# Three low-part subtractions of the attention output weights, on GpSimd instead of VectorE

## The reference, cut to what matters

```
q = (h @ w_q + b_q)                      # 16 heads of 64
logits = q k^T / 8 + bias;  masked to a window of 128
m = max(logits.max(-1), sink);  p = exp(logits - m)
probs = p / (p.sum(-1) + exp(sink - m))
o = probs @ v
mix = o @ w_o + b_o                      # w_o: 1024 x 1024
hs = hs + rms_norm(mix, norm_mix_post);  then the ffn with w_gate_up
```

## Time and profile before

| | us |
|---|---|
| median of 3 runs | 987.18 |
| lowest and highest | 986.81, 991.97 |
| the profiled execution | 991.97 |
| its span | 990.2 |
| mean granted clock of PE | 0.987 of full speed |

### The profile page before, as it was taken

One profiled execution on the slowest core, in us unless ns is written; L12 is line 12 of the kernel. 1 busy time (PEld: TensorE's weight loads), 2 busy tenths in 40 slices (PEclk: granted clock), 3 DMA queues, 4 the chain that ended last, 5 costly groups with the idle time before them and its releaser, 6 DMA issues.

```text
span 990.2 us, 16804 instructions
## 1 busy us (share of the span) xinstructions
PE 956.9 (97%) x6905; PEld 799.6 (81%) x6905; DVE 521.1 (53%) x927; ACT 413.3 (42%) x688; POOL 181.9 (18%) x246
## 2 busy tenths in 40 slices
PE   6999999999999999999999999989899999999985
PEld 5899999998978899999998999778754554554465
DVE  3645544436895655555446648774623333323266
ACT  4543333436686633434456456753311111111172
POOL 4033333111002233333120422201200000000013
PEclk8999999999999999999999999999899999999998
DMA  8444453457813344543563431129389999999901
GB/s 312 171 153 183 173 185 117 175 165 221 175 69 126 130 170 173 189 171 125 181 244 150 177 128 48 48 90 390 132 334 415 422 422 420 422 421 422 419 40 43
DMA packets 37213, 211.76 MB, mean 214 GB/s; under 512 B 2576, under 2 KB 16160, under 8 KB 18080
## 3 DMA queue, kind: packets, MB, share of 16 engines
q1 hardware_dynamic: 37152, 210.91, 55.8%
HBM read 209.83 MB, written 1.07 MB: 213 GB/s over the span
## 4 chain that ended last, share of the span: by engine, by line
PE 89%; DVE 4%; ACT 3%; issue 2%; DMA 1%; POOL 1%; SPq 0%; DVEq 0%; POOLq 0%; ACTq 0%
PE ps L1387 50%; PE ps L1861 11%; PE ps L1875 6%; PE ps L1884 3%; PE ps L1379 2%; PE ps L1833 2%; PE ps L1315 2%; PE ps L1834 2%; PE ps L1404 1%; PE ps L1538 1%; PE ps L1604 1%; PE ps L1323 1%; PE ps L1470 1%; DMA ring<-in_w_pool 1%; PE ps L1796 1%
## 5 line engine op out<-in xcount | busy, mean ns | idle before, releaser
L689 DVE TENSOR_TENSOR wl<-ring,wh 128x2048 fp32r<-128x2048 f32 (+3 forms) x103 | 204.6, 1988 | 173.6 <-ACT wh L808 173.5
L808 ACT ACTIVATE wh<-ring 128x2048 fp32r<-128x2048 f32 (+3 forms) x103 | 171.2, 1665 | 249.3 <-PE ps L1387 246.5
L1387 PE MATMUL ps<-xh,wh 128*128 128x256 f32 (+3 forms) x591 | 167.8, 284 | 0.7 <-DVE xl L2471 0.7
L1387 PE MATMUL ps<-xl,wh 128*128 128x256 f32 (+3 forms) x591 | 166.4, 282 | 0.0
L1387 PE MATMUL ps<-xh,wl 128*128 128x256 f32 (+3 forms) x591 | 166.4, 282 | 0.0
L1387 PEld LDWEIGHTS ps<-xh,wh 128*128 128x128 f32 (+3 forms) x591 | 109.3, 185 | 2.2 <-issue 1.3
L1387 PEld LDWEIGHTS ps<-xh,wl 128*128 128x128 f32 (+3 forms) x591 | 109.4, 185 | 0.1
L1387 PEld LDWEIGHTS ps<-xl,wh 128*128 128x128 f32 (+3 forms) x591 | 109.4, 185 | 0.0
L1387 PE MATMUL ps<-acth,wh 128*128 128x272 f32 (+1 forms) x352 | 100.4, 285 | 0.0
L1387 PE MATMUL ps<-acth,wl 128*128 128x272 f32 (+1 forms) x352 | 100.2, 285 | 0.0
L1387 PE MATMUL ps<-actl,wh 128*128 128x272 f32 (+1 forms) x352 | 99.9, 284 | 0.0
(11 more groups left out here) (450 smaller groups left out, 1863.3 us busy)
## 6 DMA issues: line engine op xcount, KB each, us to landing
wring<-in_w_eg SPq DMA_DIRECT2D x32, 2048.0 KB, 14.3
ring<-in_w_gu SPq DMA_DIRECT2D x22, 2048.0 KB, 7.5
wring<-in_w_ed SPq DMA_DIRECT2D x16, 2048.0 KB, 12.6
ring<-in_w_dn SPq DMA_DIRECT2D x16, 1408.0 KB, 5.8
ring<-in_w_z SPq DMA_DIRECT2D x7, 2048.0 KB, 7.6
ring<-in_w_out SPq DMA_DIRECT2D x4, 1152.0 KB, 5.1
ring<-in_w_q SPq DMA_DIRECT2D x8, 512.0 KB, 6.5
ring<-in_w_o SPq DMA_DIRECT2D x8, 512.0 KB, 15.3
```

The lines of the kernel that those rows point to most:

```text
L689: ins = dve.tensor_tensor(to, src, h.bitcast(F32), ALU.subtract)
L808: ins = act.activation(to, src, ACT.Copy)
L1387: ins = mm(o, p, q, start=first and n == 0, stop=last and n == 2)
```

## The change

`split_lo` gets a number of parts; with 8 parts a piece is made by eight subtractions of 256 columns, and the last one counts lo_done. POOL makes the low parts of w_o pieces 0, 1 and 2 in this way, after its sums for ffnpost0; it waits first until all pieces ahead of w_o are made. DVE no longer makes these three. It makes piece 3 as before, in one instruction, and waits first until lo_done has counted pieces 0 to 2.

```diff
-        def split_lo(dve, name, slot, rnd, i, j, size):
+        def split_lo(dve, name, slot, rnd, i, j, size, parts=1):
...
-            for (to, src), (h, _) in zip(parts_of(name, low, w, size), parts_of(name, high, w, size)):
-                ins = dve.tensor_tensor(to, src, h.bitcast(F32), ALU.subtract)
+            if parts > 1:
+                n = size // parts
+                for q in range(parts):
+                    at = slice(q * n, (q + 1) * n)
+                    ins = dve.tensor_tensor(low[:, at], w[:, at], high[:, at].bitcast(F32), ALU.subtract)
+            else:
+                for (to, src), (h, _) in zip(parts_of(name, low, w, size), parts_of(name, high, w, size)):
+                    ins = dve.tensor_tensor(to, src, h.bitcast(F32), ALU.subtract)
             ins.then_inc(sem("lo_done"), 1)
...
             sum_chunks(pool, "ffnpost0", T)
+            pool.wait_ge(sem("lo_done"), NUMBER["w_o", 0])
+            for x in [*halves("w_o", 0, PIECE), halves("w_o", 1, PIECE)[0]]:
+                split_lo(pool, "w_o", *x, parts=8)
             sum_chunks(pool, "mixpost1", SEQ)
...
-                if u == 2:
-                    split_lo(dve, "w_o", *halves("w_o", 0, PIECE)[0])
                 if u + 2 < HEAD_PAIRS:
                     logits(u + 2)
                 if u >= 2:
                     attended_low(u - 2)
-            split_lo(dve, "w_o", *halves("w_o", 0, PIECE)[1])
-            attended_low(HEAD_PAIRS - 2)
-            split_lo(dve, "w_o", *halves("w_o", 1, PIECE)[0])
-            attended_low(HEAD_PAIRS - 1)
+            for u in range(HEAD_PAIRS - 2, HEAD_PAIRS):
+                attended_low(u)
+            dve.wait_ge(sem("lo_done"), NUMBER["w_o", 3])
             split_lo(dve, "w_o", *halves("w_o", 1, PIECE)[1])
```

## The result

The changed kernel is slower: 997.51 us in the median of four runs (996.64 to 1000.77) beside 988.08 us for the kernel before in the same series (986.81 to 991.97). The ratio is 1.0089 with a 95% interval of 1.0065 to 1.0113. A second series, with the changed kernel timed again, gave 1.0088 (1.0064 to 1.0112). The forecast was 990.3 us, with 985.5 to 995.5 as its range. The sign was right; the forecast growth, 3.1 us, is a third of the measured 9.4 us.

A forecast was written before the change was run, and what follows sets the result against it. PE was taken to bound the attention stretch, with DVE's multiplications needed in time. Hits of 1.27 + 1.02 + 1.02 us less 0.23 us gave +3.1 us on the 987.18 us median: 990.3 us, range 985.5 to 995.5 us.

The forecast's parts named there:

- What bounds, and what the relief is worth: Attention of the first block: PE bounds; of 6.85 us taken from DVE, at most 0.23 us is gained, before logits(4).
- POOL's times, the waits and the load: POOL takes 5.9 us a piece, none late; DVE's added wait loses nothing; the earlier w_gu1 tile 1 load is booked zero.
- The hits: DVE's short instructions in pairs 0, 3 and 6 are delayed by POOL's: 1.27 + 1.02 + 1.02 us on the path.
- The price of a hit: Each DVE instruction meeting one of POOL's loses 0.36 us, the mean of two delays in the last stage.
- The upper bound that I had given: A hit on a DVE instruction costs at most 0.42 us; 24 hits on the path would cost 10.1 us.
- The cover: Slack before PE starts second heads: 0.71 us in pair 0, 0.24 us in pair 6, the latter also taken for pair 3.
- For piece 0: POOL's work from 269.9 us hits pair 0: 1.98 us of hits, 0.71 us covered, 1.27 us on the path.
- For piece 1: POOL's work from 282.6 us, four hits before pair 3's heads: 1.26 us, of which 1.02 us on the path.
- For piece 2: POOL's work from 295.9 us, four instructions fall on pair 6: 1.26 us of hits, 0.24 us covered, 1.02 us on the path.
- the granted clock of 1.00: Around the first block's attention the granted clock was read as 1.00, the 2.4 GHz level; no term was booked for it.
- Rival A: POOL holds DVE off for its whole instruction: 0.74 us a hit in pairs 0, 3 and 6, +7.8 us, 995.0 us; chance 0.20.
- Its own sign: Rival A would show as groups of four L2277 multiplications on DVE lasting over 3 us while POOL runs.

The follow-up runs named there:

- e1: The changed kernel, but POOL subtracts only 8 columns of each of the three pieces and the rest is left out; ratio to the kernel before 0.9985.
- e3: As e1 (8 columns of each piece on POOL), but w_o piece 0 whole on POOL in eight subtractions; 989.59 us, run once.
- e4: As e1 (8 columns of each piece on POOL), but w_o piece 1 whole on POOL in eight subtractions; 993.12 us, run once.
- e5: As e1 (8 columns of each piece on POOL), but w_o piece 2 whole on POOL in eight subtractions; 993.11 us, run once.
- e8: The changed kernel with 8, 6 and 3 dummy matmuls on PE before the first head of pair 3 and both of pair 6; ratio to the kernel before 1.0057.
- e6: The changed kernel with one POOL instruction of 2048 columns for each piece instead of eight; ratio to the kernel before 1.0129.

## Why the prediction was wrong, step by step

**What bounds, and what the relief is worth: right.** 6.85 us taken from DVE gave nothing in the stretch (e1), and the idle time ahead of logits(4) was 2.47 us where 2.5 was written.

**POOL's times, the waits and the load: right.** 5.6 us for a piece where 5.9 was estimated, no piece late, no wait at DVE's new semaphore. The load costs nothing by itself (e1); whether it has a share in the falls of the clock is open.

**The hits: right in place, too small in size.** The prediction had +3.3 us for the three pieces ahead of its -0.23; they cost 5.6 us with the clock at 1.00.
- The price of a hit, 0.36 us, came from rows in which a DVE instruction met one of POOL by chance. Here POOL's eight follow without a gap, and DVE's four alternate with them: 2.68 us for four is 0.67 us each, beside 0.70 us from one POOL instruction to the next. So a hit in such a series costs about POOL's 0.70 us less what the DVE instruction takes alone: 2.68 - 1.03 = 1.65 us for four multiplications, 0.41 each, and 0.33, 0.49 and 0.61 us for L2273 to L2275 behind logits(4). These three and L2286 are lines of the changed kernel. The upper bound that I had given, 0.42, was too low for the last two.
- The cover was read too large. I took 274.06 and 299.50 us from the chain of waits as the starts of the second heads of pairs 0 and 6. But PE's rows of the kernel before, here with DVE's L2215 ahead of them, give 273.89 and 299.34 us, and a first head of pair 6 that waited for L2277 already:

```profile
273.71 0.35 DVE L2215 TENSOR_SCALAR work<-sq,small 128x256 f32<-128x256 f32 x1
273.89 0.27 PE L1524 MATMUL ps<-cst,work 128*128 128x128 f32 x1
274.25 0.37 PE L1387 MATMUL ps<-xh,wh 128*128 128x256 f32 x1
298.85 0.33 PE L1524 MATMUL ps<-cst,work 128*128 128x128 f32 x1 [0.42 <-DVE work L2277]
299.34 0.30 PE L1524 MATMUL ps<-cst,work 128*128 128x128 f32 x1
```

- For piece 0, DVE's lag of 2.35 us (0.20 and 0.50 on L2273 and L2274 and 1.65 on L2286, lines of the changed kernel) met a nearer customer one step on: query(6) (L1387) waits for L2215, which was done at 274.06 us, and PE started query(6) at 274.25 us, a cover of 0.19 us where I had 0.71. The row "0.16 <-DVE work L2224" is that wait. 2.35 less 0.19 is 2.16, beside 2.21 us in e3; the prediction had 1.27.
- For piece 1 the four hits cost 0.33 + 0.49 + 0.61 + 0.28 = 1.71 us (the last is L2282 of the changed kernel, 0.43 us instead of 0.15), and e4 shows 1.73: there was no cover. For piece 2 the lag was 0.15 on L2282 and 1.65 on L2286, 1.80 us, and PE was 1.76 us late (e5): the cover was next to nothing, where the prediction took 0.24 us for each. It had 1.02 us for either piece.

**The term that is missing: PE's clock.** I noted the granted clock of 1.00 and carried it into the kernel after. In the changed kernel it fell to the 1.2 GHz level behind PE's waits. This costs 4.35 us of the 10.1 in the first profile, and 5.8 of 11.6 us in the second. In the one profile with the waits of pairs 3 and 6 filled it did not fall (e8). It is the largest part of the miss. In the stretch 3.1 us were forecast and 10.1 came: of the 7.0 us between them 4.35 are clock, and the rest is waits.

**Rival A** named the mechanism that e6 shows, and its 995.0 us was nearest to the measured time. That is in part luck: it priced a hit at 0.74 us, where the four multiplications show 0.41, and it had no clock, and the two errors offset each other. Its own sign, groups of four over 3 us, did not come (2.68). It had 0.20 because no delay in the rows was longer than 0.42 us, and rows 12 and 13 showed only 0.11. The POOL instructions of rows 13 have 128 columns and one input, and take about 0.63 us each (5.07 us for eight), hardly less than those here. So it was not their length that kept the delay small; why it was small, no run here shows.

## What to carry to other kernels

Before you give work to GpSimd, look at what VectorE does in the same microseconds, and not at how idle GpSimd is. Where that is short instructions with two SBUF inputs, or tensor_scalar from SBUF, each can be held off until GpSimd's current instruction ends, again and again in a series, and finer parts lower the price (with the clock at 1.00, 65.2 us with 64 columns and 68.2 with 256, beside 62.6 without). The whole wait until the end was seen on two-input instructions; the tensor_scalar ones were met in series of 64 and 256 columns only. And price a wait on a saturated TensorE twice: once for its length, once for the time at half clock that may follow.

## What the runs showed of the hardware that was not expected

An instruction of VectorE on 128 x 4 numbers lasted 4.28 us. The falls of the granted clock came in lengths of 3.4 and 6.8 us and differed between two executions of the same kernel (10.2 and 13.6 us low in the stretch), while PE's waits for DVE there repeated to 0.04 us. One GpSimd subtraction of 2048 columns took 4.56 us, eight of 256 took 5.62 us and 32 of 64 took 9.25 us.
